# A multi-head attention stage on one core: gating moved behind the next head's maxima, rope sums taken from PSUM, and a shorter running sum in the last head

## The reference

```python
N_HEADS_B = 8; Q_RANK = KV_RANK = 256; NOPE_DIM = 64; ROPE_DIM = 32; V_DIM = 64   # PAST_LEN = 128

q = (rmsnorm(cq, qg) @ w_uq).reshape(B, L, N_HEADS_B, NOPE_DIM + ROPE_DIM)
q = concatenate([q[..., :NOPE_DIM], apply_axial_rope(q[..., NOPE_DIM:], cos, sin)], axis=-1)
kv = (keys_c @ w_ukv).reshape(B, Lk, N_HEADS_B, NOPE_DIM + V_DIM)
k = concatenate([kv[..., :NOPE_DIM], broadcast(keys_r)], axis=-1);  v = kv[..., NOPE_DIM:]
s = einsum('bqhd,bkhd->bhqk', q, k) * ATTN_SCALE
p = softmax(s, axis=-1)
o_b = einsum('bhqk,bkhd->bqhd', p, v).reshape(B, L, D_B)
y = concatenate([y_a * silu(g_a), o_b * silu(g_b)], axis=-1) @ w_out
```

## Time and profile before

| | us |
|---|---|
| median of 3 runs | 1485.82 (1476.45 to 1486.34) |
| the profiled execution, whole | 1485.91 |
| its span, first to last instruction | 1483.8 |
| PE busy in the span | 1382.7 (93%) |
| PEld, DVE, ACT, POOL busy | 1060.0, 693.6, 412.0, 225.8 |
| granted TensorE clock, mean | 0.97 of full |

### The profile page before, as it was taken

How to read it: one execution, slowest core, us unless ns; L and a number is a source line. 1 busy time by engine, 2 the same in 40 slices (tenths; PEclk the granted TensorE clock), 3 DMA queues, 4 the chain that set the end, 5 groups by cost and what they waited for, 6 DMA issues and landing times.

```text
span 1483.8 us, 17637 instructions
## 1 busy us (share of the span) xinstructions
PE 1382.7 (93%) x6802; PEld 1060.0 (71%) x6802; DVE 693.6 (47%) x964; ACT 412.0 (28%) x731; POOL 225.8 (15%) x163
## 2 busy tenths in 40 slices
PE   6698999999999989799999999899999999999997
PEld 2597999999943446554444444488889999998786
DVE  5611314132324497867777777745322222223543
ACT  2722212111212112233334334345421111112211
POOL 1310000000012200044444445500000000000000
PEclk9898999999979999989999999999999999999999
DMA  8300333333230021400000000122310000003411
GB/s 366 136 1 33 108 125 135 118 121 131 95 142 27 29 92 43 156 6 6 1 27 0 21 0 16 66 82 86 117 31 30 30 30 30 30 30 114 170 43 57
DMA packets 29919, 107.01 MB, mean 72 GB/s; under 512 B 3660, under 2 KB 7952, under 8 KB 26417
## 3 DMA queue, kind: packets, MB, share of 16 engines
q1 hardware_dynamic: 28144, 99.30, 18.7%
q10 hardware_dynamic: 1728, 7.08, 1.2%
HBM read 89.67 MB, written 16.66 MB: 72 GB/s over the span
## 4 chain that ended last, share of the span: by engine, by line
PE 71%; DVE 15%; issue 5%; DMA 3%; POOL 2%; ACT 2%; SPq 1%; DVEq 0%; PEld 0%; POOLq 0%; ACTq 0%; PEldq 0%
PE bank L539 41%; PE bank L1008 13%; DVE amax_part L1748 3%; PE bank L866 2%; PE bank L893 2%; PE bank L762 2%; PE bank L1075 2%; POOL fw L2025 2%; DVE amax_part L1750 2%; DMA SCR<-x_sample_in 2%; DVE SCR L1719 1%; PE bank L698 1%; PE bank L550 1%; PE bank L706 1%; DVE SCR L1782 1%
## 5 line engine op out<-in xcount | busy, mean ns | idle before, releaser
L539 PE MATMUL bank<-H_r,WR_r 128*128 128x384 f32 x1728 | 352.9, 336 | 1.6 <-DVE H_r L1919 1.2
L539 PEld LDWEIGHTS bank<-H_r,WR_r 128*128 128x128 f32 x1728 | 302.7, 188 | 6.4 <-issue 4.2
L539 PE MATMUL bank<-H_r,SCR_r 128*128 128x384 f32 x480 | 161.7, 337 | 0.0
L2025 POOL TENSOR_TENSOR fw<-fw,SCR 128x1024 f32<-128x1024 f32 x56 | 142.0, 2536 | 93.1 <-ACT SCR L1363 92.0
L1363 ACT ACTIVATE SCR<-bank 128x512 f32<-128x512 f32 x144 | 82.9, 597 | 141.2 <-PE bank L866 132.9
L1989 POOL TENSOR_SCALAR ssq<-ssq 128x1 f32<-128x1 f32 (+1 forms) x36 | 16.0, 445 | 612.9 <-ACT bank L1103 514.0
L539 PE MATMUL bank<-H_r,WX_r 128*128 128x384 f32 x384 | 101.0, 344 | 3.3 <-PEq L638 3.3
L1008 PE MATMUL bank<-H_r,WR_r 128*128 128x512 f32 x432 | 99.8, 394 | 3.9 <-DVE SCR L1952 3.9
L1008 PEld LDWEIGHTS bank<-H_r,WR_r 128*128 128x128 f32 x432 | 82.2, 190 | 21.3 <-DVE SCR L1952 4.1
L1541 DVE SCALAR_TENSOR_TENSOR SCR<-bank,col,SCR 128x766 f32<-128x766 f32 (+1 forms) x96 | 43.0, 511 | 109.2 <-ACT SCR L1249 107.8
L539 PEld LDWEIGHTS bank<-H_r,SCR_r 128*128 128x128 f32 x480 | 91.0, 190 | 0.0
(11 more groups left out here) (290 smaller groups left out, 2122.1 us busy)
## 6 DMA issues: line engine op xcount, KB each, us to landing
WR<-w_mod_in SPq DMA_DIRECT2D x16, 1024.0 KB, 6.8
SCR<-w_in_in SPq DMA_DIRECT2D x20, 512.0 KB, 3.4
H<-w_mod_in SPq DMA_DIRECT2D x4, 2048.0 KB, 14.3
SCR<-x_sample_in SPq DMA_DIRECT2D x16, 512.0 KB, 14.7
WR<-w_io_in SPq DMA_DIRECT2D x16, 512.0 KB, 3.4
sp_rows<-SCR SPq DMA_DIRECT2D x9, 512.0 KB, 2.6
KV<-sp_rows SPq DMA_DIRECT2D x9, 512.0 KB, 7.8
H<-w_oe_in SPq DMA_DIRECT2D x2, 2048.0 KB, 12.5
```

The lines of the kernel that those rows point to most:

```text
L539: last = nc.tensor.matmul(out, l, r, start=(n == 0), stop=(n == len(pairs) - 1))
L2025: ptt(p_acc, pT[0] if kt == 1 else p_acc, pT[kt % 3], ALU.add).then_inc(p_added, 1)
```

## The change

Four edits, all in the attention stage:

1. In `queries`, the second product of the rope (L1717) is written in place into PSUM, and the sum (L1719) reads that PSUM region and `q` instead of two SBUF tiles. The tile `rtmp` goes.
2. `gate_output` leaves the loop over t in `maxima` and comes after `maxima`, as one function with three products (columns 0 to 511, 512 to 1,023, and the prompt's 128, which `finish_prompt` used to gate). It waits for `sg_in` where `finish_prompt` did.
3. On SyncE, `gate_load` moves behind the `max_row` that followed it, and past a `w_load_next` in the loop.
4. In head 7, GpSimd adds seven tiles (six adds) instead of nine. `row_sums` of that head then runs over `p_acc` and the last two `pT` tiles, three times two matmuls with ones that accumulate. It is moved ahead of all `first_out` matmuls and the two waits in front of them.

```diff
@@ SyncE @@
                 w_load_next(i, 2)
                 max_row(i, 2)
-                gate_load(i + 1)
                 w_load_next(i, 3)
                 max_row(i, 3)
+                gate_load(i + 1)
             max_row(HEADS // 2 - 1, 0)
+            max_row(HEADS // 2 - 1, 1)
             gate_load(HEADS // 2 - 1)
-            max_row(HEADS // 2 - 1, 1)
@@ TensorE @@
-            def row_sums(i, s):
-
-                pe.wait_ge(p_added, at(i, s, KT9 - 1, KT9 - 1 + 3))
+            def row_sums(i, s, rest=0):
+
+                pe.wait_ge(p_added, at(i, s, KT9 - 1, KT9 - 1 - rest + 3))
                 pe.wait_ge(o_cp, at(i, s, 3, 1))
-                for half in range(2):
-                    last = nc.tensor.matmul(bank[VD * half:VD * (half + 1), 2, :], ones[:, 0:VD], p_acc[:, 512 * half:512 * (half + 1)], start=True, stop=True)
+                parts = [p_acc] + [pT[kt % 3] for kt in range(KT9 - rest, KT9)]
+                for n, part in enumerate(parts):
+                    for half in range(2):
+                        last = nc.tensor.matmul(bank[VD * half:VD * (half + 1), 2, :], ones[:, 0:VD], part[:, 512 * half:512 * (half + 1)],
+                                                start=(n == 0), stop=(n == len(parts) - 1))
                 last.then_inc(sum_mm, 1)
...
+            row_sums(HEADS // 2 - 1, 1, rest=2)
             pe.wait_ge(wo_his, 12)
             pe.wait_ge(y_los, 1)
-            for k in range(2):
-                for a in range(2):
-                    first_out(k, a, wo_hi)
-            row_sums(HEADS // 2 - 1, 1)
-            for k in range(2, 6):
+            for k in range(6):
                 for a in range(2):
                     first_out(k, a, wo_hi)
@@ VectorE @@
                     tt_(q[64:96, a:a + w], bank[64:96, b, 0:w], rope_q[64:96, a:a + w], ALU.mult)
-                    link(tt_(rtmp[64:96, 0:w], bank[96:128, b, 0:w], rope_q[96:128, a:a + w], ALU.mult))
+                    link(tt_(bank[96:128, b, 0:w], bank[96:128, b, 0:w], rope_q[96:128, a:a + w], ALU.mult))
                     dve.wait_ge(pq_cp, at(i, s, 3, n + 1))
-                    tt_(q[64:96, a:a + w], q[64:96, a:a + w], rtmp[64:96, 0:w], ALU.add).then_inc(pj_q, 1)
+                    tt_(q[64:96, a:a + w], bank[96:128, b, 0:w], q[64:96, a:a + w], ALU.add).then_inc(pj_q, 1)
...
-                        elif 5 <= t < 7:
-                            gate_output(i, s - 2, t - 5)
...
                 link(nc.vector.reciprocal(rinv_prompt[0:VD, :], bank[0:VD, 2, 2 * P:3 * P]))
-                tt_(y, bank[0:VD, 2, P:2 * P], rinv_prompt[0:VD, :], ALU.mult).then_inc(o_cp, 1)
-                dve.wait_ge(o_cp, at(i, s, 3, 1))
-                dve.wait_ge(sg_in, i * 16 + 16 * (s // 2 + 1))
-                tt_(y, y, sgate[r, LS:TOK], ALU.mult)
+                tt_(out_part(i, s, LS, TOK), bank[0:VD, 2, P:2 * P], rinv_prompt[0:VD, :], ALU.mult).then_inc(o_cp, 1)
...
+            def gate_output(i, s):
+
+                dve.wait_ge(sg_in, i * 16 + 16 * (s // 2 + 1))
                 dve.wait_ge(o_cp, at(i, s, 3, 2))
+                for a, b in ((0, 512), (512, LS), (LS, TOK)):
+                    y = out_part(i, s, a, b)
+                    last = tt_(y, y, sgate[head_rows(s), a:b], ALU.mult)
+                last.then_inc(o_cp, 1)
...
                     maxima(i, n, before)
+                    if before:
+                        gate_output(i, s - 1)
@@ GpSimd @@
-                for kt in range(1, KT9):
+                for kt in range(1, tiles):
...
-            add_probs(HEADS // 2 - 1, 1)
+            add_probs(HEADS // 2 - 1, 1, KT9 - 2)
```

More of the change, by code:

```diff
@@ L223, in build @@
         w_k = [split(WR[:, 4608 + 128 * i:4736 + 128 * i], 2) for i in range(2)]
-        rtmp = WR[:, 3712:4096]
         k_hi = [WR_r[:, TOK + 1280 * i:TOK + 1280 * (i + 1)] for i in range(2)]
@@ L1767, in finish_prompt @@
             def finish_prompt(i, s):
-                r, c = slice(s % 2 * VD, (s % 2 + 1) * VD), ds1(i + (s // 2 + CA))
-                y = yT[r, c, LS:TOK].rearrange("p a n -> p (a n)")
                 dve.wait_ge(pp_mm, at(i, s, 1, 1))
                 link(nc.vector.reciprocal(rinv_prompt[0:VD, :], bank[0:VD, 2, 2 * P:3 * P]))
-                tt_(y, bank[0:VD, 2, P:2 * P], rinv_prompt[0:VD, :], ALU.mult).then_inc(o_cp, 1)
-                dve.wait_ge(o_cp, at(i, s, 3, 1))
-                dve.wait_ge(sg_in, i * 16 + 16 * (s // 2 + 1))
-                tt_(y, y, sgate[r, LS:TOK], ALU.mult)
+                tt_(out_part(i, s, LS, TOK), bank[0:VD, 2, P:2 * P], rinv_prompt[0:VD, :], ALU.mult).then_inc(o_cp, 1)
             def reciprocals(i, s, *parts):
@@ L1787, in head_rows, with out_part @@
                 return slice(s % 2 * VD, (s % 2 + 1) * VD)
-            def out_half(i, s, half):
-                return yT[head_rows(s), ds1(i + (s // 2 + CA)), 512 * half:512 * (half + 1)].rearrange("p a n -> p (a n)")
+            def out_part(i, s, a, b):
+                return yT[head_rows(s), ds1(i + (s // 2 + CA)), a:b].rearrange("p a n -> p (a n)")
             def normalise_output(i, s, half):
                 h = slice(VD * half, VD * (half + 1))
-                last = tt_(out_half(i, s, half), bank[h, 6 + s % 2, :], rinv[h, :], ALU.mult)
+                last = tt_(out_part(i, s, 512 * half, 512 * (half + 1)), bank[h, 6 + s % 2, :], rinv[h, :], ALU.mult)
                 if half:
                     last.then_inc(o_cp, 1)
-            def gate_output(i, s, half):
+            def gate_output(i, s):
+                dve.wait_ge(sg_in, i * 16 + 16 * (s // 2 + 1))
                 dve.wait_ge(o_cp, at(i, s, 3, 2))
[L1802 to L1805, removed]
+                for a, b in ((0, 512), (512, LS), (LS, TOK)):
+                    y = out_part(i, s, a, b)
+                    last = tt_(y, y, sgate[head_rows(s), a:b], ALU.mult)
+                last.then_inc(o_cp, 1)
             def finish(i, s):
@@ L1810, in finish @@
                     normalise_output(i, s, half)
-                for half in range(2):
-                    gate_output(i, s, half)
+                gate_output(i, s)
             def attend(i, s, before=True, after=True):
@@ L2016, in _, with add_probs @@
             ptt(yp[:, 1, :], pr[:, 2, :], pr[:, 3, :], ALU.add).then_inc(yp_made, 1)
-            def add_probs(i, s):
-                for kt in range(1, KT9):
+            def add_probs(i, s, tiles=KT9):
+                for kt in range(1, tiles):
                     pool.wait_ge(st_exp, at(i, s, UNITS, unit(kt, 1) + 5))
```

## The result

The changed kernel took 1492.11 us in the median of 8 runs (1482.38 to 1500.19), the kernel before 1480.34 in the median of 8 beside it (1476.45 to 1486.34). The ratio is 1.0083, 95% interval 1.0054 to 1.0111: 12 us slower, where 7 us faster was forecast. The profiled execution took 1500.19 us with a span of 1498.3; it is the longest of the eight, and the trace of the kernel before is of one of its longer executions too (1485.91 us).

What follows compares the result with a forecast made beforehand. TensorE, busy 93% of the span, was taken as the bound, with VectorE setting the pace in the maxima. Edits -7.8 + 0 + 0 + 0.9 = -6.9 on a 1483.8 span, plus 2.1 around it: 1479.0 us, range 1469.5 to 1484.5.

Steps and rivals of the forecast that it cites:

- Everything behind it on VectorE stands where it stood: Maxima, t = 0: locked behind GpSimd's third add, the first query remainder still ends at 813.71, so edit 1 gains 0.
- the prediction's last sentence: Loop and head 7: prediction wrong if L1725 takes 0.56 us, L902 waits for L1773 or TensorE's clock falls in the loop.
- the 65 ns estimated for each sum: Rope sums: reading PSUM instead of SBUF makes each some 65 ns longer, still under the 1.07 us cover.
- the worst case's working: VectorE's hole behind the maxima: gate products alternating with GpSimd's adds take 6.5 us, hidden with 1.0 us to spare.
- the cold case: Head 7: row sums' twelve passes run at half clock, 5.9 us; +0.9 taken, bounds -1.9 and +2.2.
- the rope gain comes too: Start of the maxima: L1725 is not held or GpSimd's add comes later; 6.4 us more gained, 1472.6; chance 0.12.
- The rival on the slower side: Behind the maxima: moved gates hold back the row sums; 8.2 us lost with one more add, 1487.2; chance 0.03.
- The quicker execution: Whole kernel: it falls more often into the execution seen 9.4 us below the others, 1469.6; chance 0.12.

Runs made afterwards that it cites:

- e1: The changed kernel with its rope lines (edit 1) as before; ratio 0.9951 to the kernel before, median 1468.78 us.
- e2: The kernel before with the rope edit (edit 1) alone; ratio 1.0114 to the kernel before, median 1499.44 us.
- e5: The changed kernel with the first matmul of the fifth key tile's scores repeated four times in heads 0 to 6; ratio 0.9895 to the kernel before.
- e9: The kernel before with the rope edit and four repeated matmuls before the fifth key tile's scores; ratio 0.9971 to the kernel before, median 1473.53 us.
- e3: The kernel before with edits 2 and 3 alone (gates behind the maxima, gate load moved); ratio 0.9954 to the kernel before, median 1470.17 us.
- e6: The changed kernel with the first query remainder moved from t = 0 to t = 1 of the maxima; ratio 0.9833 to the kernel before.
- e4: The kernel before with head 7's edit (edit 4) alone; ratio 0.9992 to the kernel before, median 1475.90 us.
- e7: The changed kernel without the rope edit, first query remainder moved to t = 1; ratio 0.9875 to the kernel before, median 1461.52 us.
- e8: The kernel before with only the first query remainder moved from t = 0 to t = 1; ratio 0.9962 to the kernel before, median 1472.13 us.

## Why the prediction was wrong

**The term that failed is edit 1, put at 0 per head.** Its working held nearly to the digit: the sum at 0.43 us, TensorE about a microsecond earlier, the first remainder locked until the add lets go, VectorE where it stood. The step that failed is the next one, from "Everything behind it on VectorE stands where it stood" to "I price edit 1 at 0 per head": it leaves out TensorE. A TensorE that runs 1.07 us ahead of an unchanged VectorE stands those 1.07 us still later, next to a wait that is there already. I asked what is late next, and not in how long a piece the idle time then lies. The waits of 0.90 and 0.41 us became one of 1.62, and where the clock stayed full the head was no longer for it (39.33 us, 39.26 in e1). After this piece the clock fell in four heads of six, and a head with a fall took 5.9 us more than one without. Edit 1 cost 17 us alone (e2), 20 with the others (the change against e1). e2 shows that the edit does this alone, e5 and e9 that it is the standstill and the clock, not the lock. Its bounds, "0 and 6 x 1.07 = 6.4 us" gained, excluded a loss without a reason. That the clock could fall in a head of the loop stands in the prediction's last sentence, but with no price and no chance, and so the range ended 7.6 us below the median. That the in-place product might cost more was covered: it took 20 ns more than the write to SBUF (448 for 428 ns, 581 for 561) and the sum from PSUM 12 ns more than from SBUF (561 for 549), so the 65 ns estimated for each sum were not seen.

**The starting point was high.** The forecast of 1479.0 starts from 1485.9, the median of three runs; the median of eight beside the change is 1480.34. From there -6.9 us would have given about 1473.

**Edit 2 was right.** 7.8 us forecast; e3 gave 0.9954, 6.8 us of 1477.6 (3.7 to 9.9 by its interval), and the heads went from 40.8 to 39.3, against 39.4. Six times that is 8.7 us, a little over the upper bound of 8.2. The gates behind the maxima took 5.87 us where VectorE had a hole of 3.9 (the worst case's working had 6.5); `finish_prompt` came right behind them and the row sums waited for nothing (e6). The Trainium skill, SBUF — State Buffer, section Who interferes with whom, has the engine that issues second wait for the whole instruction of the first; the trace agrees, with two adds of GpSimd inside those 5.87 us.

**Edit 3** was hidden: no row in e3 waits for the gate load.

**Edit 4** had the right mechanism and the wrong sign: +0.9 taken, 0.9 gained in e4's profile, 1.2 less by its ratio, which can't be told from 0. I took the cold case whole, and the clock was at half for only a part of the row sums. (The cold sums' end was 0.5 us behind 952.13 by its own rows, not 0.7; that changes little.)

**The rival "the rope gain comes too"** was worth 6.4 us by its working and 1.2 us per head once nothing was locked (e6 against e7), but not in this kernel. **The rival on the slower side** named the gates; e3 rules it out. **The quicker execution** of the kernel before was not explained in the prediction, and no trace shows one. The traces of the other kernels point ahead of head 1: where the line of e6 is not moved and nothing is repeated, the attention's first scores lie at 628.4 to 629.4 us and head 0 takes 41.1 to 42.2 in three traces (the kernel before, the change, e4), and at 621.8 to 624.7 and 39.8 to 40.0 in the other three (e1, e2, e3). What makes the difference stays open. The low clock in head 0 can only be a part of it: e8, whose trace has none there, still spreads over 8.5 us.

**Not settled:** why the clock falls after the same standstill in four heads and not in the other two. It is not tied to one of the two kinds of head. The traces, one per kernel, show only that it never fell in heads 1 to 6 where TensorE's longest wait for VectorE in them was 1.1 us or less (the kernel before, e1, e3 to e9), and that it fell in four of six heads with 1.6 us (the change, e2). Nothing between 1.1 and 1.6 us was tried.

## What to carry to other kernels

When an edit makes the bounding engine wait less in one place, follow it to the place where it waits next, and ask whether two waits now lie together: here the length of TensorE's single standstill counted, and not only the sum. Where GpSimd works beside VectorE, list the VectorE operations with two SBUF inputs (and SBUF copies) against GpSimd's running times, and move those that nobody waits for into the gaps; here one line gave 0.4% in the kernel before and turned a change 0.8% slower into one 1.7% faster. If the waits can't be taken away, extra matmuls in them whose result is overwritten can be cheaper than the fallen clock (e5 against the change, 1.9%).

## What the runs showed of the hardware that I had not expected

A standstill of TensorE of 1.6 us was followed by a fall of its clock to the 1.2 GHz level in four heads of six, for 3 to 10 us. In the long heads of the change the late scores moved GpSimd's fifth add by 0.9 us, over a VectorE operation that had been nearly clear of it; VectorE came 0.9 us later by that, a second operation fell under the sixth add, and the next standstill and the next fall followed. An SBUF copy of 640 columns took 0.48 us alone and 2.36 under an add of GpSimd, while the reductions of 768 columns out of PSUM took at most 0.96 in either place. The Trainium skill, SBUF — State Buffer, section Who interferes with whom, counts such copies among the operations that can contend and the reductions not, and the trace agrees with both.
